# Half-level interleaving of a delta rule's inverse in 64-wide tiles, and earlier gates, pooling and transposes, in a three-layer FP32 block

## The reference, cut to what matters

```python
# even mixer, delta rule: 8 heads, chunks of c = 64 tokens
q, k = l2norm(q) * dk ** -0.5, l2norm(k)
lower = where(strict, (k * beta) @ k.T * decay, 0)      # per head and chunk, 64 x 64
tmat = lower + eye(c)
u = solve(tmat, v * beta); w = solve(tmat, kb * exp(g))
# scan over the chunks: v_new, o, state
o_gdn = rms_norm(o, onorm_w) * silu(z)
mixed = concat([stick_breaking(q, k, v), o_gdn]) @ w_out

# second block
proj = rmsnorm(h) @ w_in                                # pool_in, pool_gate, ssm_in, ssm_gate
ya = pool_mixer(pool_in) * silu(pool_gate)              # running means over 2, 4, 8, 16 tokens
y = ssm(ssm_in); hg = gelu(y) @ w_glu
yb = hg[:, :1024] * sigmoid(hg[:, 1024:]) * silu(ssm_gate)
h = h + concat([ya, yb]) @ w_out
h = h + (p @ w_ple) * sigmoid(h @ w_ple_gate)
out = rmsnorm(h)
```

## Time and profile before

| | |
|---|---|
| median of three runs | 2982.25 us (2982.09 to 2982.33) |
| the profiled execution's own time | 2980.04 us |
| its span, first to last instruction | 2978.3 us |
| granted TensorE clock, mean | 0.993 of 2.4 GHz |
| TensorE busy (matmul) | 2897.8 us, 97% |
| VectorE busy | 1649.8 us, 55% |
| ScalarE busy | 1410.5 us, 47% |
| DMA, HBM | 173 GB/s over the span |

### The profile page before, as it was taken

The page is one execution under the profiler, slowest core; times in us unless marked ns, Lnnn a source line. Parts: engine busy times, 40 slices in busy tenths (PEclk is TensorE's granted clock), DMA queues, the critical chain, the costliest instruction groups (busy, mean ns, idle before and its releaser), DMA issues.

```text
span 2978.3 us, 36439 instructions
## 1 busy us (share of the span) xinstructions
PE 2897.8 (97%) x14602; PEld 2407.5 (81%) x14602; DVE 1649.8 (55%) x2038; ACT 1410.5 (47%) x1802; POOL 25.2 (1%) x43
## 2 busy tenths in 40 slices
PE   8999999999999999999999999999999999999998
PEld 6878878788888888878887878888888887887876
DVE  5775656545544444564444554554454567876545
ACT  5543366544444444454446454444444445454444
POOL 0000000000000000000000000000000000000000
PEclk9999999999999999999999999999999999999999
DMA  6532245465655655556552555555555654445543
GB/s 235 183 128 85 85 141 189 161 207 184 196 188 194 194 187 190 187 173 198 184 190 78 198 194 184 184 195 195 188 193 186 198 192 141 148 144 172 185 155 127
DMA packets 255842, 516.77 MB, mean 174 GB/s; under 512 B 8528, under 2 KB 8752, under 8 KB 254688
## 3 DMA queue, kind: packets, MB, share of 16 engines
q1 hardware_dynamic: 252896, 501.61, 51.1%
q0 software_dynamic: 2816, 13.33, 1.4%
HBM read 511.76 MB, written 2.10 MB: 173 GB/s over the span
## 4 chain that ended last, share of the span: by engine, by line
PE 92%; DVE 4%; ACT 3%; issue 1%; DMA 0%; SPq 0%; ACTq 0%; DVEq 0%
PE acc L474 84%; PE side L672 2%; ACT ar L1116 1%; DVE ar L1804 1%; PE side L541 1%; DVE wlo L1816 1%; PE side L783 1%; PE side L567 1%; ACT whi L1127 0%; DVE ar L1807 0%; DMA raw<-in_ev_w_in 0%; ACT L1116 0%; PE side L927 0%; PE side L967 0%; PE side L936 0%
## 5 line engine op out<-in xcount | busy, mean ns | idle before, releaser
L1816 DVE TENSOR_TENSOR wlo<-raw,whi 128x1024 fp32r<-128x1024 f32 x948 | 1154.5, 1224 | 1150.5 <-ACT whi L1127 1149.9
L1127 ACT ACTIVATE whi<-raw 128x1024 fp32r<-128x1024 f32 x948 | 998.0, 1060 | 1199.9 <-PE acc L474 1199.0
L474 PE MATMUL acc<-whi,xh 128*128 128x512 f32 x3008 | 822.4, 395 | 6.5 <-ACT whi L1127 5.2
L474 PE MATMUL acc<-wlo,xh 128*128 128x512 f32 x3008 | 806.7, 390 | 0.4
L474 PE MATMUL acc<-whi,xl 128*128 128x512 f32 x3008 | 806.3, 390 | 0.0
L474 PEld LDWEIGHTS acc<-wlo,xh 128*128 128x128 f32 x3008 | 564.9, 188 | 121.8 <-DVE wlo L1816 3.7
L474 PEld LDWEIGHTS acc<-whi,xl 128*128 128x128 f32 x3008 | 565.8, 188 | 119.7
L474 PEld LDWEIGHTS acc<-whi,xh 128*128 128x128 f32 x3008 | 556.6, 189 | 117.9 <-issue 6.2
L474 PE MATMUL acc<-whi,hTh 128*128 128x512 f32 x784 | 212.3, 393 | 5.8 <-DVE ar L1804 3.1
L474 PE MATMUL acc<-whi,hTl 128*128 128x512 f32 x784 | 211.0, 391 | 0.0
L474 PE MATMUL acc<-wlo,hTh 128*128 128x512 f32 x784 | 210.6, 390 | 0.1
(11 more groups left out here) (259 smaller groups left out, 1211.9 us busy)
## 6 DMA issues: line engine op xcount, KB each, us to landing
raw<-in_ffn_w_gate SPq DMA_DIRECT2D x88, 1024.0 KB, 5.1
raw<-in_ffn_w_up SPq DMA_DIRECT2D x88, 1024.0 KB, 5.1
raw<-in_ffn_w_down SPq DMA_DIRECT2D x88, 1024.0 KB, 5.0
raw<-in_ev_w_in SPq DMA_DIRECT2D x56, 1024.0 KB, 5.1
raw<-in_od_w_in SPq DMA_DIRECT2D x48, 1024.0 KB, 5.2
raw<-in_w_in SPq DMA_DIRECT2D x32, 1024.0 KB, 5.3
raw<-in_ev_w_out SPq DMA_DIRECT2D x16, 1024.0 KB, 5.1
raw<-in_od_w_out SPq DMA_DIRECT2D x16, 1024.0 KB, 5.0
```

Source lines behind the costliest of these rows:

```text
L474: mm = pe.matmul(acc[2 * pair + t][:], x[:, k0 + j, t * P:t * P + P], w[:, ring, j], start=start and j == 0, stop=stop and j == 1)
L1127: act.activation(whi[:, place % RING], raw_granule(place), ACT.Copy).then_inc(S("hi_done"), 1)
L1816: dve.tensor_tensor(wlo[:, place % RING], raw_granule(place), whi[:, place % RING].bitcast(F32), ALU.subtract).then_inc(S("lo_done"), 1)
```

## The change

It does six things. (1) The products of levels 1 to 5 go in two 64x64 tiles on the diagonal, rows and columns 0 to 63 and 64 to 127 (`mm4_halves`); VectorE subtracts the two diagonal quarters only. (2) The two token tiles go half a level apart: step n of 13 does the first product of one tile and the second ones of the other, and a granule follows while `half_gap(hg, n)` is 1: 11 granules in the first head group, 10 in the second, for 6 and 6. (3) `turn` of `ev_sb` uses freed `acc` banks. TensorE's part of `sb_stage(0)` comes after the delta rule; one granule of `ev_sb` is then left. (4) `glu` takes gate, value, gate, value. (5) `pool_group` moves to `s_in` (granules 57, 59, 61, 63), with other scratch, and the pool matmuls to granules 4, 6, 8, 10 of `glu`. (6) Transposes for `s_out` go into `glu` (rounds 0 to 5) and before its third granule (6, 7), those for `pg` into the last chunk of `s_out` (0 to 5) and between granules of `ple` (6, 7), and the copies of `ple`'s results go between the splits.

```diff
-POOL_AT = [7, 9, 11, 13]
+POOL_AT = [4, 6, 8, 10]
+POOLED_AT = [57, 59, 61, 63]
+HALF_AT = {11: (0, 1), 12: (2,), 13: (3,), 14: (4,), 15: (5,)}
+GATE_AT = {3: (0, 1), 4: (2,), 5: (3,), 6: (4,), 7: (5,)}
...
-            "glu": (kview(A["w_glu_2"][0]), [0, 1024, 512, 1536]),
+            "glu": (kview(A["w_glu_2"][0]), [1024, 0, 1536, 512]),
...
+        def half_gap(hg, s):
+            return int(s < 11 - hg)
...
+                    elif name == "ev_sb":
+                        b = claim(acc[2 * ((CHUNK0[name] + c) % 2) + j], "turn_done", n + 1 - 12)
...
-                if (c, j) == (5, 6):
-                    sb_stage(0)
...
+            def mm4_halves(bank, lhs, rhs):
+                for k in range(4):
+                    for g in range(2):
+                        o = slice(64 * g, 64 * g + 64)
+                        mm = pe.matmul(bank[o, k * P + 64 * g:k * P + 64 * g + 64], lhs(k)[o, o], rhs(k)[o, o],
+                                       start=True, stop=True)
                 return mm
...
-                for l in range(1, 7):
-                    for t in range(TT):
-                        ...
-                    beside()
+                def first_product(l, t):
+                    U = lambda k: unit(t, k)
+                    product = mm4_halves if l < 6 else mm4
+                    pe.wait_ge(S(f"inv_step{t}"), 31 * hg + (5 if l == 1 else 5 * l - 2))
+                    b = claim(side[t], f"T_done{t}", 6 * hg + l)
+                    product(b, lambda k: U(LM_)[:, k], lambda k: U(M_)[:, k]).then_inc(S("t1_ready"), 1)
+                def second_products(l, t):
+                    ...
+                for n in range(13):
+                    if n < 12:
+                        first_product(n // 2 + 1, n % 2)
+                    if n:
+                        second_products((n - 1) // 2 + 1, (n - 1) % 2)
+                    beside(half_gap(hg, n))
...
+            sb_stage(0)
             for _ in sb_granules:
...
+                if 4 * c + j in HALF_AT:
+                    to_features("s_out", u, HALF_AT[4 * c + j])
...
             def s_out_aside(c, j):
+                if c == 0 and j == 2:
+                    to_features("s_out", u, (6, 7))
+                if c == 3 and j in GATE_AT:
+                    to_features("pg", h, GATE_AT[j])
...
             next(ple_granules)
             next(ple_granules)
-            to_features("pg", h)
+            to_features("pg", h, (6,))
+            next(ple_granules)
+            to_features("pg", h, (7,))
...
             for c in range(4):
                 split(gran("ple", c))
-                if c == 2:
-                    lead()
+                if c < 3:
+                    features_hi("pg", (3 + c,))
+                if c >= 2:
+                    ple_out(c - 2)
+            features_hi("pg", (6, 7))
...
+                    if l < 6:
+                        masked(l + 1, t)
+                        dve.wait_ge(S("p_ready"), ready + 1)
+                        for g in range(2):
+                            o = slice(64 * g, 64 * g + 64)
+                            x = unit(t, M_)[o, :, o]
+                            tt(x, x, four(side[t][:])[o, :, o], sub, inv)
```

More of the change, by code:

```diff
@@ L1193, in turn_out @@
                     act.wait_ge(S("turned"), n + 1)
-                    run(turned_to(name, c, j), side[j][:], ACT.Copy, "turn_done")
+                    b = acc[2 * ((CHUNK0[name] + c) % 2) + j] if name == "ev_sb" else side[j]
+                    run(turned_to(name, c, j), b[:], ACT.Copy, "turn_done")
             def features_hi(name, rounds=range(8)):
                 base = 8 * TOF[name]
-                if name != "ev_gdn":
-                    act.wait_ge(S("used"), GRAN0["ple" if name == "pg" else name])
+                if name == "s_out":
+                    act.wait_ge(S("used"), GRAN0["glu"])
+                elif name not in ("ev_gdn", "pg"):
+                    act.wait_ge(S("used"), GRAN0[name])
                 for r in rounds:
+                    if name == "pg":
+                        act.wait_ge(S("used"), gran("s_out", 3, r) + 1)
                     act.wait_ge(S("tof_ready"), base + r + 1)
@@ L1732, in lead @@
             def lead():
-                glu_out(3)
-                features_hi("s_out")
+                features_hi("s_out", (5, 6, 7))
             def s_out_aside(c, j):
+                if c == 3 and j >= 5:
+                    features_hi("pg", (j - 5,))
                 if (c, j) == (2, 4):
@@ L1744, in _, with ple_out @@
             linear("s_out", lambda c: None, lead, s_out_aside)
-            def lead():
-                features_hi("pg")
-            for c in range(4):
-                split(gran("ple", c))
-                if c == 2:
-                    lead()
-            for c in range(4):
+            def ple_out(c):
                 act.wait_ge(S("used"), gran("ple", c) + 1)
@@ L1757, in _ @@
                     run(u[:, t, c * CH:c * CH + CH], acc[2 * pair + t][:], ACT.Copy, "ple_out")
+            for c in range(4):
+                split(gran("ple", c))
+                if c < 3:
[3 more added lines that the diff above has]
+            features_hi("pg", (6, 7))
             def gate_out(c):
@@ L2518, in gate_lo, with pool_group, step @@
                    steps(gate_h[:, 2 * e:2 * e + 2]).bitcast(F32), sub, "gl_done")
+            def pool_group(g):
+                def step(o, a, b, op):
+                    work(o, a, b, op)
+                    own()
+                if g == 0:
+                    dve.wait_ge(S("turn_done"), 2 * TURN["s_in", 3] + 2 - 12)
+                    dve.wait_ge(S("turned"), 2 * TURN["s_in", 3] + 2)
+                    dve.wait_ge(S("y_ready"), 8)
+                v = at(PT, 8, TOK)[:, 2 * g:2 * g + 2]
+                src = v
+                if g:
+                    dve.wait_ge(S("pooled"), g)
+                for k in range(g + 1):
+                    o = (pc[:, SLOT:SLOT + CH] if k % 2 else at(ZS, CH)).rearrange("p (a n) -> p a n", a=2)
+                    step(o[:, :, 1 << k:], src[:, :, 1 << k:], src[:, :, 0:TOK - (1 << k)], ALU.add)
+                    step(o[:, :, 0:1 << k], src[:, :, 0:1 << k], src[:, :, 0:1 << k], ALU.max)
+                    src = o
+                inv = pc[:, g * TOK:(g + 1) * TOK].unsqueeze(1).to_broadcast([P, 2, TOK])
+                step(src, src, inv, ALU.mult)
+                tt(grow[:, CH * g:CH * g + CH].rearrange("p (a n) -> p a n", a=2), src, v, ALU.subtract, "pooled")
             def s_aside(c, j):
```

155 lines of the change are left out of this document (77 added, 78 removed).

## The result

| | before | changed |
|---|---|---|
| median of four runs | 2982.17 us (2980.68 to 2982.33) | 2950.52 us (2949.33 to 2950.87) |
| span of the profiled execution | 2978.3 us | 2947.5 us |
| granted TensorE clock, mean | 0.993 | 0.993 |

The ratio is 0.9894, with a 95% interval of 0.9877 to 0.9911: 31.7 us less. The forecast was 2952, the range 2944 to 2961. The span is 30.8 us shorter where the sum said 30.1.

The account below looks back on a forecast made before the run. The prediction took TensorE, busy 97% of the span, as the bound. Terms of -15.5 - 4.8 - 1.3 + 0.3 - 8.8 = -30.1 us against 2980.04 gave 2949.9, forecast as a median of 2952 us, range 2944 to 2961.

Parts of the forecast that it names:

- Narrow products: Inverse: 60 products at 0.505 instead of 0.898 us, -23.6 us; turning in and out of the narrow form, +2.8 us.
- the delta part: Delta rule through attention start: -15.5 us in all; the rival that it gives nothing, 2967 us, had chance 0.05.
- Waits that go: Delta rule: TensorE's waits for `turn_out`, T and `turn` vanish, 1.4 us left at the second group's first level: -7.1 us.
- New waits: Last steps of the inverse, without granules: 2.5 us in the first group, 0.45 and 1.6 in the second, together +4.6 us.
- End of the delta rule: The delta rule's end moves by +1.2 us, from 376.82 to 378.0, with nine granules (+24.5 us) put ahead of it.
- The chain: Attention: stage 0 starts at 385.3, not 402.46, -17.2 us; new TensorE wait of 8.2 us, slow clock behind it +1.7.
- `glu`: Gate first removes chunk 2's wait for its bank, slow clock included: -4.8 us; window groups cost nothing in either place.
- `s_out`, `ple`, `pg`: Transposes moved earlier: `s_out` -1.3 us and +0.3 for three more places; `ple` and `pg` -8.8, one 0.25 us wait left.
- The late part: Everything from glu on, glu, s_out, ple and pg together: 14.6 us less by the forecast's terms.
- VectorE's pace: Rival, chance 0.06: narrow subtractions cost 0.68 us, so VectorE paces the inverse; about +6 us, 2958 us.
- the granted clock was 1.00: Rival, chance 0.03: the clock falls after narrow work in the inverse, 1.7 us for each of 21 steps; +35 us, 2987.
- the tiles did run side by side: Its opposite was a rival, chance 0.03: narrow tiles don't overlap, a product takes 1.28 us, +46 us, 2998 us.

Follow-up runs that it names:

- e1: The changed kernel with four full 128x128 matmuls in every product of the inverse instead of the narrow ones: 2969.59 us.
- e9: Inverse, its granules, `turn` and `sb_stage(0)` as before the change, only glu, pooling, s_out, ple and pg as changed: 2965.3 us.
- e3_gap_even: The changed kernel with a granule only after every other step of the inverse, 6 in each head group: 2949.24 us.
- e6: The changed kernel with the granules of `ev_z` on the other attention stages, one stage later on all three engines: 2950.38 us.
- e12: The changed kernel plus early first-tile normalisation, no granules in second-group steps 1 and 5, ScalarE's root earlier, two VectorE splits later: 2945.01 us.
- e10_three_behind: The changed kernel with no granule in the second group's steps 1, 4 and 7, so three more lie behind the delta rule: 2947.46 us.
- e4: The changed kernel with the chunks of glu in the order value, gate, value, gate again: 2957.0 us.
- e5: The changed kernel with VectorE normalising the second head group's first token tile before the delta rule's last output: 2948.21 us.

## Why the prediction was right

It was right step by step. The single terms were off by about a microsecond, in both directions, and that they nearly cancelled (30.8 for 30.1) is luck.

- **Narrow products.** Confirmed: -20.8 with the turns by my terms, 19 to 20 when undone. They carry the delta part; the rest of it costs 3 to 5 us by e1 and e9. The sum has this too, but I didn't see it. A step takes 4.49 us, 0.05 to 0.1 more than summed, over 20 steps 1 to 2 us.
- **Waits that go.** No wait for out `h` is left. The first level of the second group waits 2.13 us, where I left 1.4. One wait that I had not listed, 0.5 us in the first group's `turn`, went too.
- **New waits.** 2.05 + 1.36 + 1.38 = 4.8 us for 4.6, though not in the parts that I gave.
- **End of the delta rule.** 378.85 for 378.0; the levels had begun 0.35 later. Of the terms above, those that were too small make more than this difference; I did not place the remaining us.
- **The chain.** Stage 0 at 386.36 for 385.3, stage 1 at 393.43 for 392.4, the wait 7.97 for 8.2: the delay of the delta rule's end, handed on. The slow clock behind it cost 16.11 - 15.25 = 0.86 us (from the last stage, 474.87 before and 459.62 now), not 1.7: I took the price from a whole granule, and here the first 2.7 us at 1.2 GHz were short products, after which the stage waited for VectorE anyway. Together -15.2 for -15.5.
- **`glu`.** Right in kind, and the window groups cost nearly nothing in either place (3.3 and 3.0 us to the free bank). In the changed kernel the order is worth 6.4, more than my 4.8, since it also spares the wait behind `glu`, which my sum didn't have.
- **`s_out`, `ple`, `pg`.** One wait of 0.18 us is left, where I had 0.25. `pg`'s features are worth 9.0 for 8.8. The late part was -15.6 for -14.6; 6.6 of it are left for `glu` and `s_out`, where I had 5.8. The transposes for `s_out` and the place of the pooling have no run of their own.

**VectorE's pace** was the rival that I held for the likeliest. VectorE of the changed kernel in order of time, its four subtractions of a step:

```profile
211.46 1.77 DVE L1850 TENSOR_TENSOR ar<-ar,side 64x256 f32<-64x256 f32 x4 [2.17 <-PE side L685]
```

And the group of all of them, by form (busy, mean ns of one, idle before):

```profile
L1850 DVE TENSOR_TENSOR ar<-ar,side 64x256 f32<-64x256 f32 x80 | 33.5, 419 | 18.5 <-PE side L685 16.5
```

One takes 419 ns, the time of 256 elements, whether on 64 partitions or on 128. A step has 3.7 us of VectorE work under 4.49 of TensorE's. The cover is thin: where a step has no granule, TensorE waits the 0.60 us seen in e3_gap_even. The other rivals: stage 1 moved by 16 us, so the delta part gave what it should; the granted clock was 1.00 from 205 to 211 us, and from 211 to 250 and from 310 to 380 us too; and the tiles did run side by side, at 32.3 ns an instruction.

## What to carry to other kernels

A wait that an engine gains at a landmark must be priced from the chain that releases it: measure from the last input to the landmark, and ask what moves that interval. Filling the wait from behind moved no stage and gave 1.7 us at the most (e6); moving work there out of an earlier place, together with an order on the other engines that lets the chain start at once, gave 6.5 us of span (e12). And a part of a change that looks like its idea can be a cost on its own: only the run that takes the narrow products out showed where the gain was (e1 beside e9). And when work is moved behind a point, the helpers' part of it, splits and roots on other engines, is moved too, and may land ahead of the very chain that it should cover.

## What the runs showed of the hardware

**Two tiles side by side.** In the changed order each FP32 matmul's two instructions are followed by two on the other quarter: half of the neighbours differ. In turn, 2 of 16 do. If a neighbour on the same quarter costs s and one on the other d, 32.3 = (s + d) / 2 and 42.5 = (14 s + 2 d) / 16 give s = 46 and d = 19 ns (an estimate of a two-price model, not tested further; whether the weight loads or the matmuls overlap isn't shown). The Trainium skill, TensorEngine Tiling (Array Packing), Gotcha 1, has different row tiles unable to access one PSUM bank at the same time; here both tiles write the same bank, from rows 0 to 63 and 64 to 127, and the alternating order is the faster one, so these traces don't bear it out for this pair.

**The same wait, two clocks.** At 205 us TensorE stands for 2.1 us in every one of these kernels, and behind it the granted clock differs from one trace to the next. The stretch from 205 to 211 us in the changed kernel and in e10_three_behind, which are the same program up to there:

```profile
205.00:211.00 6.00, 5.14 (x60) 4.29 (x62) 4.28 (x6) 1.18 (x2) 0.00 (x0) 1.00 0.18 34
```

```profile
205.00:211.00 6.00, 5.99 (x38) 5.03 (x38) 3.43 (x4) 0.60 (x1) 0.00 (x0) 0.72 0.33 96
```

1.00 in the one, 0.72 in the other, and 38 matmuls instead of 60 in the same 6 us. The second step begins at 210.98 us in e10 for 210.26, although its first level had begun 0.85 us earlier (205.01 for 205.86): 1.6 us lost. e1, e4, e5 and e6 show 0.72 there as well. In the five with 0.72 the first level began at 205.01 to 205.46 us, in the eight with 1.00 at 205.41 to 205.96; I did not find what decides it. It is one reason why whole traces stand 1 to 2 us apart. Another lies behind the stages: the kernel before and e9 are the same program up to `glu`, stand 0.1 us apart at the last stage (474.87 and 474.78) and 1.15 us apart at the start of `glu` (2704.79 and 2705.94). So small effects have to be read as intervals within one trace.
